# Layer 1's mixer phase: value and key block of the first attention head in places three and four

## The reference

```python
h = rmsnorm_2(x, norm1_g) * (1.0 + sc1) + sh1
hc = rmsnorm_2(xc, norm1_g) * (1.0 + sc1c) + sh1c
a, mq, mk, mv, mo, mg, dq, dk, dv = jnp.split(h @ w_in, splits, axis=-1)
ac, mqc, mkc, mvc, moc, mgc, dqc, dkc, dvc = jnp.split(hc @ w_in, splits, axis=-1)
conv_l = conv_module(a, ...)          # GLU of a, 31 taps over time, layer norm, silu
mlstm_l, _ = mlstm_mixer((mq, mk, mv, mo, mg), ...)   # 4 heads, forwards and backwards
diff_l, _ = diff_mixer((dq, dk, dv), ...)             # 4 heads of two softmaxes each
mix = jnp.concatenate([conv_l, mlstm_l, diff_l], axis=-1)
x = x + g1 * (mix @ w_out)
```

## Time and profile before

| what | value |
|---|---|
| median of 3 runs | 3812.93 us (3812.8 to 3814.53) |
| the profiled execution | 3814.33 us, its span 3812.5 us |
| mean granted TensorE clock | 0.986 |
| TensorE busy | 3707.4 us, 97% |
| VectorE, ScalarE, GpSimd busy | 2453.5, 1656.2, 994.9 us |
| layer 1's mixer phase | from about 2725 to 2940 us of the span |

### The profile page before, as it was taken

One profiled execution on the slowest core, in us unless ns is written; L12 is line 12 of the kernel. 1 busy time (PEld: TensorE's weight loads), 2 busy tenths in 40 slices (PEclk: granted clock), 3 DMA queues, 4 the chain that ended last, 5 costly groups with the idle time before them and its releaser, 6 DMA issues. The chain is left out here.

```text
span 3812.5 us, 66366 instructions
## 1 busy us (share of the span) xinstructions
PE 3707.4 (97%) x24018; PEld 3317.0 (87%) x24018; DVE 2453.5 (64%) x4691; ACT 1656.2 (43%) x2980; POOL 994.9 (26%) x462
## 2 busy tenths in 40 slices
PE   9999999999899999999999999999898999999998
PEld 8788799876799999888799999888777899998887
DVE  7641344276459789556578898556654597895555
ACT  4344043233345444455444444555533454444554
POOL 4554055095059000000086000000280590000000
PEclk9999999999899999999999999999998999999999
DMA  7667755321145444555554444555411454445554
GB/s 267 235 221 270 238 173 179 124 72 45 53 161 180 139 149 146 184 192 186 182 172 163 147 146 154 193 186 193 146 67 50 150 176 141 148 150 182 193 193 144
DMA packets 172292, 618.43 MB, mean 162 GB/s; under 512 B 18832, under 2 KB 22288, under 8 KB 172048
## 3 DMA queue, kind: packets, MB, share of 16 engines
q1 hardware_dynamic: 171904, 614.82, 48.0%
q10 hardware_dynamic: 144, 0.28, 0.0%
HBM read 613.98 MB, written 1.05 MB: 161 GB/s over the span
## 5 line engine op out<-in xcount | busy, mean ns | idle before, releaser
L2349 ACT ACTIVATE ring_hi<-ring 128x1024 fp32r<-128x1024 f32 x786 | 832.6, 1059 | 503.1 <-PE bank L2278 503.1
L2221 PE MATMUL bank<-H_r,ring_hi 128*128 128x256 f32 x3248 | 939.8, 289 | 11.5 <-POOL ring_r L2206 6.5
L2223 PE MATMUL bank<-H_r,ring_r 128*128 128x256 f32 x3248 | 921.7, 284 | 0.0
L2222 PE MATMUL bank<-H_r,ring_hi 128*128 128x256 f32 x3248 | 921.5, 284 | 0.0
L289 POOL TENSOR_TENSOR ring_r<-ring,ring_hi 128x1024 fp32r<-128x1024 f32 x169 | 412.2, 2441 | 1704.1 <-ACT ring_hi L283 1050.7
L2221 PEld LDWEIGHTS bank<-H_r,ring_hi 128*128 128x128 f32 x3248 | 625.7, 193 | 14.3 <-issue 5.6
L2222 PEld LDWEIGHTS bank<-H_r,ring_hi 128*128 128x128 f32 x3248 | 626.2, 193 | 0.0
L2223 PEld LDWEIGHTS bank<-H_r,ring_r 128*128 128x128 f32 x3248 | 625.1, 192 | 0.0
L2206 POOL TENSOR_TENSOR ring_r<-ring,ring_hi 128x1024 fp32r<-128x1024 f32 x156 | 432.2, 2795 | 327.2 <-ACT ring_hi L2349 327.2
L2274 PE MATMUL bank<-ring_hi,w_high 128*128 128x512 f32 x1536 | 476.5, 391 | 1.8 <-DVE ring_r L2593 1.8
L2593 DVE TENSOR_TENSOR ring_r<-ring,ring_hi 128x1024 fp32r<-128x1024 f32 x390 | 474.7, 1218 | 2.6 <-ACT ring_hi L2349 2.5
(11 more groups left out here) (406 smaller groups left out, 5665.5 us busy)
## 6 DMA issues: line engine op xcount, KB each, us to landing
ring<-in_peer_u SPq DMA_DIRECT2D x384, 512.0 KB, 3.2
ring<-in_peer_v SPq DMA_DIRECT2D x384, 512.0 KB, 3.3
ring<-in_w_in SPq DMA_DIRECT2D x135, 512.0 KB, 3.4
arena<-in_ada SPq DMA_DIRECT2D x96, 512.0 KB, 5.4
ring<-in_w_f SPq DMA_DIRECT2D x72, 512.0 KB, 3.4
ring<-in_w_br SPq DMA_DIRECT2D x24, 512.0 KB, 4.1
ring<-in_w_out SPq DMA_DIRECT2D x24, 512.0 KB, 3.2
ring<-in_w_q SPq DMA_DIRECT2D x24, 512.0 KB, 3.2
```

The source lines that it names most:

```text
L2221: pe.matmul(o, hi[:, k], x_hi_[:, kt, :], start=(kt == 0), stop=False)
L2222: pe.matmul(o, hi[:, k], x_lo_[:, kt, :], start=False, stop=False)
L2223: mm = pe.matmul(o, lo[:, k], x_hi_[:, kt, :], start=False, stop=(kt == KT - 1))
L2349: act.activation(ring_hi[:, m % NH, :], ring[:, (n0 + m) % NS, :], ACT.Copy).then_inc(a_hi, 1)
```

## The change

In layer 1, behind gate 0 and mv 0 now come dv 0 and dk 0 (places 2 and 3); sig 0 and sig 1 go to places 4 and 5, glu 0 and glu 1 to 6 and 7, dq 0 to 8. From place 9 on (mk 0) the order is as before. `ctx_blocks` goes from 2 to 3, so gate 0, mv 0 and dv 0 are begun with the context half; `tiled` stays 3. The tables of slots, the step b = 5 of ScalarE and the b >= 7 of GpSimd stay.

```diff
--- before.py
+++ after.py
@@ -139,7 +139,7 @@
     conv = [("sig", 0), ("sig", 1), ("glu", 0), ("glu", 1)]
     first = [("gate", 0)]
     if l == LAYERS - 1:
-        first.append(cell[0].pop(0))
+        first += [cell[0].pop(0), diff[0].pop(0), diff[0].pop(1)]
     return first + conv + diff[0] + cell[0] + diff[1] + diff[2] + cell[1] + diff[3] + [("mo", 0), ("mo", 1)]
 
 
@@ -1425,7 +1425,7 @@
             nb = len(names)
             fresh_of = {b: j for j, b in enumerate(b for b in range(nb) if names[b][0] in ("mv", "dv"))}
             places = {"sig": u_sig, "mq": mq, "mk": mk, "mo": mo, "dq": dq, "dk": dk}
-            ctx_blocks, tiled = (2, 3) if last else (4, 1)
+            ctx_blocks, tiled = (3, 3) if last else (4, 1)
             evac = ["dve" if n in ("gate", "glu") else "act" for n, _ in names]
 
             def at(name, i):
```

## The result

The changed kernel takes 3819.61 us (median of 12 runs, 3816.31 to 3822.49), the kernel before, run beside it, 3813.57 us (12 runs, 3810.46 to 3817.14). The ratio is 1.0017, with a 95% interval of 1.0009 to 1.0025: slower by 6.0 us (the interval runs from about 3.4 to 9.5 us). Forecast were 3816.0 us in a range of 3810.5 to 3819.0. The direction came as predicted, and the size is about twice the 3.1 us of the sum, just outside the range. The profiled execution took 3820.72 us with a span of 3818.9.

What follows compares the result with a forecast made beforehand. TensorE, busy 97% of the span, was taken as the bound. Shortened and moved waits, low clock in block 7 and new GpSimd waits netted +3.1 us at block 9: 3816.0 us on the median's scale, range 3810.5 to 3819.

Steps and rivals of the forecast that it cites:

- It only moves the end of block 0 by 2.9 us: Start of layer 1's mixer phase: the third context half, 24 matmuls, covers no wait and delays block 0's end by 2.9 us.
- The wait ahead of block 5: TensorE ahead of block 5, for GpSimd's low part: a wait of 1.5 us instead of 3.5.
- the one in slot 13: TensorE at the gate state's transposes: waits for v_state at 2761.9 and ScalarE's exponential; block 7 starts at 2763.0.
- the wait ahead of block 8: TensorE behind block 7: GpSimd's first tap now precedes low part 8, so block 8 starts 5.3 us after block 7 ends.
- The rotation: VectorE's rotation of head 0, behind its later taps: work ends at 2780.1, rotation asked at 2784.4, covered by 4 us.
- moves with them: Share wait of 2.2 us behind the scores: a chain through VectorE and ScalarE that shifts with the scores.
- left it at 1.00: TensorE's clock at the 2.2 us gap, stage from 2787 to 2790: full clock, unlike the gaps of 3.49 and 3.81 us.
- a stage after 2800 that has changed by more than it was moved: Listed sign that the prediction is wrong, for the stages of the phase after 2800 us; no size given.
- both engines are released together: VectorE's scans and GpSimd's low parts, both released by ScalarE's softplus: the 6 us lost in 12.8 us of scans stay.
- Full clock in block 7: Rival at block 7: the gap, broken by transposes, doesn't lower the clock; +0.4 us, 3813.3; chance 0.33.
- The faster one: Rival at the scans: they no longer meet low parts, v_state comes up to 6 us earlier; -3.2 us, 3809.7; chance 0.08.
- The slower one: Rival at block 9: the gap ahead of block 8 keeps the clock low into it; +10.0 us, 3822.9; chance 0.06.

Runs made afterwards that it cites:

- before3: Kernel before, old order, with three blocks begun with the context half instead of two (24 matmuls added): 3815.65 us, ratio 1.0008.
- tok15: Changed kernel with the turn of the gate state in slot 15 instead of 13: 3811.60 us, ratio 0.9998.
- taps9: Changed kernel with GpSimd's taps begun behind block 9 instead of block 7: 3815.57 us, ratio 1.0006.
- taps8: Changed kernel with GpSimd's taps begun behind block 8 instead of block 7: 3816.09 us, ratio 1.0009.
- skip14: Changed kernel without GpSimd's two taps behind block 14, computed at the end of its list: 3817.96 us, ratio 1.0017.
- skip1: Changed kernel with one GpSimd tap behind block 14 instead of two, the last moved to the end of its list: 3816.95 us, ratio 1.0015.
- three_two: Changed kernel (new order, three blocks begun) with two blocks side by side in the latent half instead of three: 3812.99 us, ratio 0.9997.
- two_begun: Changed kernel (new order) with two blocks begun and two side by side instead of three and three: 3808.53 us, ratio 0.9987.
- before22: Kernel before, old order, two blocks begun, with two side by side in the latent half instead of three: 3808.78 us, ratio 0.9992.
- again: Changed kernel measured again without any edit: 3818.82 us, ratio 1.0018 of the kernel before.
- all3: Changed kernel with two begun, two side by side, gate state turned in slot 15 and GpSimd's taps from block 9: 3802.99 us, ratio 0.9976.

## Why the prediction was right and wrong

**The start.** "It only moves the end of block 0 by 2.9 us": right; VectorE reads it at 16.8 in place of 13.9 us, and in before3, which has this alone, at 16.8 too.

**Blocks 5 to 8.** The wait ahead of block 5 was 1.3 us (1.5 forecast), the one in slot 13 3.06, block 7 ran at 1.2 GHz and ended at about 43.7 us (43.6), the wait ahead of block 8 was 5.53 us (5.3). These terms stand. (The 3.40 us that were read for "two halves and the turn" are one half and the turn; with the half more the 6.1 us are right.) GpSimd idled 11.8 us ahead of its first tap, where some 9 were forecast. tok15 and taps9 took the two waits away one at a time, and each uncovered the next that the code has.

**Blocks 8 and 9.** Block 9 came at 55.6 in place of 55.1: 0.3 us came with block 8, and I had costed GpSimd's step at 6.2 us, where 6.4 lie between low parts 8 and 9 (2768.53 to 2774.91). The rotation, which I called covered, added 0.4 us. First scores: +3.1 forecast, +4.1 measured.

**The step that failed** is the last one: the share wait of 2.2 us "moves with them", and with it all that stands behind. I had read that this wait "left it at 1.00", the clock. So the clock behind that wait was put at nothing, from one trace of the kernel before, and the stage cited for it (2787 to 2790) even ends ahead of the end of the wait at 2790.47; the stages behind read 1.00 too, but in that trace. The first scores are not where the account closes. From there to the end mark the traces of the changed kernel gained another 3.0 us twice and 6.0 once. In slot 21 the same wait had a low clock behind it, 1.6 us to the second scores, in all three. These 1.6 us moved TensorE and VectorE against GpSimd, whose train stood where it had stood, and so the share product of slot 31 began behind a low part and was held: 1.5 us more wait, and 1.4 to 2.9 us of low clock behind it. Two of the three traces got 1.5 us back, as they have no low clock behind a wait of 1.51 us near the end where all three of the kernel before have one. The sum closes: 1.6 + 1.5 + 2.9 = 6.0 for the first trace, 1.6 + 1.5 + 1.4 - 1.5 = 3.0 for the others.

This accounts for the traces. The medians (6.0, and 5.5 in the second session) lie a little under them, and their interval reaches down to 3.4 us, so the 4.1 us at the first scores alone would lie within it too. My list named "a stage after 2800 that has changed by more than it was moved" as a sign of error, and it is the one that came.

I had the mechanism of the hold in hand, in the scans: there I wrote that both engines are released together and the overlap stays as it is. That was right for the scans, and at the first scores too, where GpSimd's low part stands 1.64 us behind in both kernels. It fails wherever TensorE and VectorE are slowed and GpSimd isn't. One slip in the chances: the cases that pass 7.6 us above are the slower rival and half of the others, 0.07 and not 0.05.

**The rivals.** Full clock in block 7: no. The faster one (the scans no longer meet the low parts) did not come; taps8 and taps9 show its mechanism from the other side, with 2.0 us for each low part. The slower one, a clock that stays low into block 9, had the right agent and the wrong place: the low clock filled block 8 but was gone by block 9 (1.00 from 2778), and came again at blocks 11 and 16. skip14 and skip1 did have one in block 9 (0.53 in the stage from 2784 in skip1), at the price of about 1 us.

**Where the loss comes from.** At an equal end of block 0 (three_two) or with two and two (two_begun against before22) the order costs nothing that these intervals show. What is left for the loss is the 24 matmuls, 2.9 us, that now stand ahead of block 0's end and hide nothing there; three_two has the third context half too, and gives them back on the latent side. Both orders answer to them: by 3.3 us in the old one (before3), by 4.3 in the new one (from 1.2 to 5.5 us over the kernel before, three_two to again), where each distance is good to about 3.5 us. Clear of noise is the step that moves 48 matmuls behind block 0's end, two_begun against again in one session: 10.3 us. In the traces the end mark moves by 7.2 us in the old order (209.6 to 216.8), by 3.5 in the new one. What more there is to gain stands behind GpSimd's taps, v_state in slot 13 and VectorE's taps; with those moved and two begun, all3 is 9.4 us under the kernel before (3803.0 against 3812.4), of which before22 has 3.6 in the old order. How much of the rest is the order's was not tried.

**The rule that the prediction drew on.** The Trainium skill, page "SBUF — State Buffer", section "SBUF: two separate sides", has the loser of the shared port pair wait for the whole instruction of the other. These runs agree: 2.31 to 2.35 us for a share product of 0.3 us that starts 0.1 us behind a low part of 2.34 us. The section names VectorE instructions with two SBUF inputs or in a two-port mode; whether the share product, with one tensor input, is in that mode, no run tests; they show only that it is held. Weighed only at the scans, it changed nothing in the sum; applied to each slot behind, it would have widened the range upwards by some 2 us for each product that is waited for.

**Open.** When the clock falls: gaps of 2.2 us had a low clock behind them in six of twelve traces, in either order, and the same program up to that place had it in the three of the changed kernel and not in skip14 and skip1. So the larger part of what failed, the clock in slot 21 and what followed from it, is read from the traces and not brought about by an edit; no run takes it away by itself. And of the spread of the times, some 10 us, most seems to lie ahead of this phase, whose start varies by 9 us; what varies there was not looked at.

## What to carry to other kernels

Work put ahead of a chain is paid unless the engine waits in that place, and when a producer moves, look for who is queued behind the instruction that waits for it: here the weight preparation behind the convolution's taps. A clock that falls behind a wait can cost twice, as in slots 21 and 31 here: once in the matmuls, and again when the engines that it slows meet another that it doesn't slow. So one trace without a low clock behind a wait is no ground for costing it at nothing, and a sum that closes at the first common mark should leave a few microseconds for what stands behind.

## What was not expected of the hardware

A wait of 0.91 us of TensorE, between small matmuls, was followed by a clock of 1.2 GHz (PEclk 0.63 in its stage, skip1), while one of 2.2 us was not in six traces of twelve. Three traces of the kernel before agreed to 0.1 us at all marks, although their phases started up to 2 us apart in the span, and two of the changed kernel with the same waits differed by 3.0 us, through the clock alone.
